# Two-layer encoder trunk on one core: weights of one recurrent output chunk by GpSimd alone, a join in pairs, a mean over four tiles

## The reference, cut to what matters

```
for i in range(2):
    a = rmsnorm(h, g[0])
    m = retention_mixer(a) if i == 0 else rglru_mixer(a)
    h = h + rmsnorm(m, g[1])
    f = conv_ffn(rmsnorm(h, g[2]))
    h = h + rmsnorm(f, g[3])
```

## Time and profile before

| what | us |
|---|---|
| median of 3 runs | 717.61 (717.42 to 718.76) |
| profiled execution, its time | 717.85 |
| profiled execution, its span | 716.0 |
| PE busy in the span | 704.6 |
| DVE busy | 607.3 |
| ACT busy | 520.2 |
| POOL busy | 25.0 |

### The profile page before, as it was taken

One profiled execution on the slowest core, in us unless ns is written; L12 is line 12 of the kernel. 1 busy time (PEld: TensorE's weight loads), 2 busy tenths in 40 slices (PEclk: granted clock), 3 DMA queues, 4 the chain that ended last, 5 costly groups with the idle time before them and its releaser, 6 DMA issues.

```text
span 716.0 us, 16121 instructions
## 1 busy us (share of the span) xinstructions
PE 704.6 (98%) x6542; PEld 589.9 (82%) x6542; DVE 607.3 (85%) x820; ACT 520.2 (73%) x848; POOL 25.0 (3%) x28
## 2 busy tenths in 40 slices
PE   9999999999999999999999999999899999999996
PEld 6788787878899888888889998888788888885464
DVE  6969877777889799989898889898999999999643
ACT  7566675857576789778777677899668888988431
POOL 0010010101010000000002300000000000000000
PEclk9999999999999999999999999999999999999999
DMA  9873363452683356555589963100525666766821
GB/s 309 318 234 120 119 235 119 166 188 104 211 274 121 111 192 225 192 195 200 176 264 388 370 216 117 62 1 1 196 98 190 224 206 207 233 211 207 275 43 59
DMA packets 106396, 132.08 MB, mean 184 GB/s; under 512 B 12385, under 2 KB 74337, under 8 KB 106209
## 3 DMA queue, kind: packets, MB, share of 16 engines
q1 hardware_dynamic: 105904, 130.97, 54.4%
q10 hardware_dynamic: 432, 0.31, 0.2%
HBM read 129.17 MB, written 1.05 MB: 182 GB/s over the span
## 4 chain that ended last, share of the span: by engine, by line
PE 82%; DVE 8%; ACT 6%; DMA 2%; issue 1%; SPq 1%; DVEq 0%
PE ps L1653 22%; PE ps L1655 22%; PE ps L1654 22%; PE ps L2036 3%; PE ps L2037 3%; PE ps L2035 3%; DMA stage<-in_ret_w_in 2%; PE ps L1696 1%; PE ps L1700 1%; PE ps L1695 1%; DVE a_lo L1082 1%; SPq L495 1%; PE ps L1901 1%; DVE hT L1098 1%; DVE w_lo L1036 1%
## 5 line engine op out<-in xcount | busy, mean ns | idle before, releaser
L1653 PE MATMUL ps<-a_hi,w_hi 128*128 128x272 f16 (+1 forms) x1000 | 276.9, 277 | 0.1
L1654 PE MATMUL ps<-a_lo,w_hi 128*128 128x272 f16 (+1 forms) x1000 | 276.9, 277 | 0.0
L1655 PE MATMUL ps<-a_hi,w_lo 128*128 128x272 f16 (+1 forms) x1000 | 276.9, 277 | 0.0
L1036 DVE SCALAR_TENSOR_TENSOR w_lo<-stage,w_hi 128x1024 f16<-128x1024 f32 x207 | 246.5, 1221 | 34.3 <-ACT w_hi L579 34.0
L579 ACT ACTIVATE w_hi<-stage 128x1024 f16<-128x1024 f32 x207 | 208.5, 1044 | 30.6 <-PE ps L2037 18.3
L1653 PEld LDWEIGHTS ps<-a_hi,w_hi 128*128 128x128 f16 x1000 | 97.8, 98 | 17.3 <-DVE rs L1045 0.9
L1655 PEld LDWEIGHTS ps<-a_hi,w_lo 128*128 128x128 f16 x1000 | 97.8, 98 | 16.0
L1654 PEld LDWEIGHTS ps<-a_lo,w_hi 128*128 128x128 f16 x1000 | 97.8, 98 | 15.7
L1653 PE MATMUL ps<-y_hi,w_hi 128*128 128x272 f16 (+3 forms) x496 | 106.1, 242 | 0.0
L1654 PE MATMUL ps<-y_lo,w_hi 128*128 128x272 f16 (+3 forms) x496 | 106.1, 242 | 0.0
L1655 PE MATMUL ps<-y_hi,w_lo 128*128 128x272 f16 (+3 forms) x496 | 106.0, 242 | 0.0
(11 more groups left out here) (278 smaller groups left out, 1104.2 us busy)
## 6 DMA issues: line engine op xcount, KB each, us to landing
stage<-in_ffn_w_in SPq DMA_DIRECT2D x96, 512.0 KB
stage<-in_ffn_w_out SPq DMA_DIRECT2D x24, 1024.0 KB
stage<-in_ret_w_in SPq DMA_DIRECT2D x16, 1024.0 KB
stage<-in_ret_w_out SPq DMA_DIRECT2D x8, 1024.0 KB
stage<-in_lru_w_in SPq DMA_DIRECT2D x8, 1024.0 KB
stage<-in_ret_w_in SPq DMA_DIRECT2D x12, 512.0 KB
stage<-in_lru_w_out SPq DMA_DIRECT2D x8, 512.0 KB
stage<-in_lru_w_a SPq DMA_DIRECT2D x8, 256.0 KB
```

Of the source, the lines that this page charges most:

```text
L1036: dve.scalar_tensor_tensor(out=part(1, c, q), in0=flat(stage, c, q), scalar=W_SCALE, in1=part(0, c, q), op0=ALU.mult, op1=ALU.subtract).th ...
L1653: pe.matmul(o, w_h, x_h, start=start, stop=False)
L1654: pe.matmul(o, w_h, x_l, start=False, stop=False)
L1655: return pe.matmul(o, w_l, x_h, start=False, stop=stop)
```

## The change

**Weights.** The four quarters of chunk `LRU_OUT` leave ACT's and DVE's `prep`. GpSimd makes them behind its last sum, in three instructions a quarter: the staged weights times 64 in place, a copy to f16 (high part), a subtraction (low part). Of the eight removed lines `prep(LRU_OUT, q)` one is shown below. GpSimd counts its quarters in a semaphore of its own, `pool_low`, on which PE waits for this chunk and SP for the load of `FFN1_IN`, the next user of that staging buffer. For this SP's loop over the chunks of the second FFN begins one round later, and the first round is written out. `whi_made` and `wlo_made` stay in step since the first quarter of `LRU_OUT + 1` adds five instead of one.

**Sum of four tiles.** In `residual_parts(1)` DVE leaves out the last two adds of squares, and the mean of the input norm of the recurrent layer sums tiles 0, 1, 4 and 5 on PE, in four products instead of one.

**Join in pairs.** In `residual(2, ...)` the output tiles are scaled by their gains on ACT, all eight, and the join goes in groups of one, one, two, two and two tiles in plain order.

```
+GROUPS = ((0, 1), (1, 1), (2, 2), (4, 2), (6, 2))
...
+        def counted(c, q):
+            return SUB + 1 if (c, q) == (LRU_OUT + 1, 0) else 1
...
+                        if isinstance(i, int) and c - 2 == LRU_OUT:
+                            sp.wait_ge(pool_low, 2 * half + 2)
+                        else:
+                            sp.wait_ge(wlo_made, SUB * (c - 2) + 2 * half + 2 + 2 * SUB * i)
...
+                if layer:
+                    for b in range(2):
+                        load_pair(first_in + b, ffn_w_in[layer], b * 2 * P, FFN + b * 2 * P)
+                with sp.Fori(layer, FFN_CHUNKS // 2) as i:
...
-            prep(LRU_OUT, 0)
...
+            def out_scaled(half, n):
+                act.activation(mT[:, half * 4 + n, T0_LRU_OUT:T], ps[:, (X, Y)[half] + n, T0_LRU_OUT:T], ACTF.Copy,
+                               scale=gain(5, half * 4 + n)).then_inc(m_part, 1)
             out_squares(LRU_OUT + 1, 2, 0, T0_LRU_OUT, 2)
-            out_squares(LRU_OUT + 1, 2, 1, T0_LRU_OUT)
+            out_scaled(0, 0)
+            out_scaled(0, 1)
+            out_square(LRU_OUT + 1, 2, 1, 0, T0_LRU_OUT)
+            out_scaled(0, 2)
+            out_square(LRU_OUT + 1, 2, 1, 1, T0_LRU_OUT)
+            out_scaled(0, 3)
+            out_square(LRU_OUT + 1, 2, 1, 2, T0_LRU_OUT)
+            out_square(LRU_OUT + 1, 2, 1, 3, T0_LRU_OUT)
+            for n in range(3):
+                out_scaled(1, n)
             estimate(STAT, T0_LRU_OUT, ms_up, MEAN[("post", 2)], ESTIMATE[("post", 2)])
+            out_scaled(1, 3)
...
-                link(dve.tensor_tensor(four, four, sq[:, 6:8, :], ALU.add))
-                link(dve.tensor_tensor(two, two, four, ALU.add))
-                dve.tensor_tensor(sq_sum[:], sq[:, 0, :], sq[:, 1, :], ALU.add).then_inc(sum_h, 1)
+                if i == 1:
+                    dve.tensor_tensor(four, four, sq[:, 6:8, :], ALU.add).then_inc(sum_h, 1)
...
+                for g in range(len(GROUPS) + 1):
+                    if g < len(GROUPS):
+                        dt, count = GROUPS[g]
+                        some = slice(dt, dt + count)
+                        dve.wait_ge(m_part, i * DT + dt + count)
+                        link(dve.tensor_tensor(mT[:, some, t0:T], mT[:, some, t0:T],
+                                               rs[:, t0:T].unsqueeze(1).to_broadcast([P, count, T - t0]), ALU.mult))
+                        dve.tensor_tensor(hT[:, some, t0:T], hT[:, some, t0:T], mT[:, some, t0:T],
+                                          ALU.add).then_inc(h_new, count)
+                    if g:
+                        before_dt, count = GROUPS[g - 1]
+                        for dt in range(before_dt, before_dt + count):
+                            norm_low(i + 1, dt, dt, t0)
...
-            out_scale(2, T0_LRU_OUT)
...
+            for q in range(SUB):
+                pool.wait_ge(w_landed[LRU_OUT % 2][q // 2], landed(LRU_OUT))
+                pool.wait_ge(w_used, freed(LRU_OUT, q))
+                raw = flat(stage, LRU_OUT, q)
+                link(pool.tensor_scalar(raw, raw, W_SCALE, None, ALU.mult))
+                link(pool.tensor_copy(part(0, LRU_OUT, q), raw))
+                pool.tensor_tensor(part(1, LRU_OUT, q), raw, part(0, LRU_OUT, q), ALU.subtract).then_inc(pool_low, 1)
...
+                        for dt in (0, 1, 4, 5):
+                            mm = pe.matmul(ps[:, STAT_IN[i], :T], ones_sb[:, 0, :], sq[:, dt, :], start=dt == 0, stop=dt == 5)
+                        mm.then_inc(ms_up, 1)
...
-                    pe.wait_ge(m_scaled, i + 1)
+                    pe.wait_ge(m_part, i * DT + 1)
...
+                    if c == LRU_OUT:
+                        pe.wait_ge(pool_low, q + 1)
```

More of the change, by code:

```diff
@@ L578, in prep @@
                     act.wait_ge(w_used, freed(c, q) + 2 * SUB * i)
-                act.activation(part(0, c, q), flat(stage, c, q), ACTF.Copy, scale=W_SCALE).then_inc(whi_made, 1)
+                act.activation(part(0, c, q), flat(stage, c, q), ACTF.Copy,
+                               scale=W_SCALE).then_inc(whi_made, counted(c, q))
             def estimate(bank, t0, up, n_up, n):
@@ L597, in norm_input @@
             def norm_input(i, t0, weights_after=()):
-                for n, dt in enumerate(JOIN_ORDER):
-                    act.wait_ge(h_new, (i - 1) * DT + n + 1)
+                for dt in range(DT):
+                    act.wait_ge(h_new, (i - 1) * DT + dt + 1)
                     high(i, dt, t0)
                     act.activation(sq[:, dt, t0:T], hT[:, dt, t0:T], ACTF.Square).then_inc(h_sq, 1)
-                    if n in weights_after:
-                        prep(FFN1_IN + 1, weights_after.index(n))
+                    if dt in weights_after:
+                        prep(FFN1_IN + 1, weights_after.index(dt))
             def norm_tokens():
@@ L1036, in prep @@
                 dve.scalar_tensor_tensor(out=part(1, c, q), in0=flat(stage, c, q), scalar=W_SCALE, in1=part(0, c, q),
[L1037 removed]
+                                         op0=ALU.mult, op1=ALU.subtract).then_inc(wlo_made, counted(c, q))
             def rsqrt(to, bank, t0, n):
@@ L1059, in out_scale @@
             def out_scale(i, t0):
-                for dt in range(4 if i < 2 else 2):
+                for dt in range(4):
                     dve.wait_ge(m_sq, i * DT + dt + 1)
-                    last = dve.tensor_scalar(mT[:, dt, t0:T], ps[:, (FULL + [X])[i] + dt, t0:T], gain(2 * i + 1, dt), None,
+                    last = dve.tensor_scalar(mT[:, dt, t0:T], ps[:, FULL[i] + dt, t0:T], gain(2 * i + 1, dt), None,
                                              ALU.mult)
@@ L1119, in residual_parts @@
                 dve.wait_ge(h_sq, (i + 1) * DT + 6)
-                mark(dve.tensor_tensor(two, two, sq[:, 2:4, :], ALU.add))
+                added = mark(dve.tensor_tensor(two, two, sq[:, 2:4, :], ALU.add))
                 part_low(i, 1, 3)
+                after(added)
                 dve.wait_ge(h_sq, (i + 2) * DT)
-                link(dve.tensor_tensor(four, four, sq[:, 6:8, :], ALU.add))
-                link(dve.tensor_tensor(two, two, four, ALU.add))
-                dve.tensor_tensor(sq_sum[:], sq[:, 0, :], sq[:, 1, :], ALU.add).then_inc(sum_h, 1)
+                if i == 1:
+                    dve.tensor_tensor(four, four, sq[:, 6:8, :], ALU.add).then_inc(sum_h, 1)
+                else:
+                    link(dve.tensor_tensor(four, four, sq[:, 6:8, :], ALU.add))
+                    link(dve.tensor_tensor(two, two, four, ALU.add))
+                    dve.tensor_tensor(sq_sum[:], sq[:, 0, :], sq[:, 1, :], ALU.add).then_inc(sum_h, 1)
@@ L1738, in chunk_normed @@
                 wh, wl = weights(c)
[L1739 to L1742, removed]
+                for k in range(KC):
+                    if k % 2 == 0:
+                        pe.wait_ge(wlo_made, SUB * c + k // 2 + 1)
+                    pe.wait_ge(ahi_made, NORM_BASE[i] + k + 1)
                     for n in range(4):
-                        if (at, n) == (0, 3):
-                            pe.wait_ge(h_new, (i - 1) * DT + 2)
                         col = slice(n * P, (n + 1) * P)
-                        pe.matmul(ps[:, X + n, t0:T], wh[:, k, col], a_hi[:, k, t0:T], start=at == 0, stop=False)
+                        pe.matmul(ps[:, X + n, t0:T], wh[:, k, col], a_hi[:, k, t0:T], start=k == 0, stop=False)
                         pe.matmul(ps[:, X + n, t0:T], wl[:, k, col], a_hi[:, k, t0:T], start=False, stop=False)
-                    pe.wait_ge(alo_made, NORM_BASE[i] + at + 1)
+                    pe.wait_ge(alo_made, NORM_BASE[i] + k + 1)
                     for n in range(4):
                         mm = pe.matmul(ps[:, X + n, t0:T], wh[:, k, n * P:(n + 1) * P], a_lo[:, k, t0:T],
[L1752 to L1755, removed]
+                                       start=False, stop=k == KC - 1)
+                    if k % 2 == 1:
                         mm.then_inc(w_used, 1)
@@ L1994, in _ @@
                         pe.wait_ge(gt_out, 2)
-                    pe.wait_ge(wlo_made, SUB * c + q + 1)
+                    if c == LRU_OUT:
+                        pe.wait_ge(pool_low, q + 1)
+                    else:
+                        pe.wait_ge(wlo_made, SUB * c + q + 1)
                     if half == 0:
```

12 lines of the change are left out of this document (2 added, 10 removed).

## The result

The changed kernel takes 730.73 us (median of 4 runs, 729.84 to 732.87) against 718.18 us for the kernel before on the same chip (4 runs): a ratio of 1.0179, 95% interval 1.0165 to 1.0194. The forecast was 728.0 us, slower, range 717.0 to 734.0. The profiled execution took 729.84 us, its span 727.8, which is 11.8 more than before.

A forecast was written before the change was run, and what follows sets the result against it. A late DVE in 423 to 447 us, then ACT from 455.44, was taken to bound the kernel. GpSimd's work with the four-tile sum +10.0, the second FFN's join +0.4: 717.6 + 10.4 = 728.0 us, range 717.0 to 734.0.

The forecast's parts named there:

- GpSimd's work in the join: First FFN's join: GpSimd's reads block DVE's two-input instructions, last a_lo 9.2 us late; gates +10.0 us including the four-tile sum.
- The price of a scaling: GpSimd's one-input scaling of 1024 f32 columns in place, taken as 1.09 us, between DVE's 0.72 and 2.34.
- my own rule: In the join, a blocked DVE loses GpSimd's working part: 0.9 us per scale or copy, 2.15 per subtraction.
- The 0.9 us that the prediction quotes for a one-input instruction: Estimate for 1024 columns on GpSimd, from the Trainium skill's 1.03 cycles a column at 1.2 GHz.
- Behind the join: From last a_lo to gates: late PE, mean and estimate, then GpSimd's remaining instructions; 9.2 us late becomes 10.0.
- Four-tile sum: Recurrent layer's input norm: PE's mean ends 1.35 us later, gates start 0.9 us late.
- Join: Ahead of the second FFN: PE waits some 0.5 us for a_lo of tiles 1 and 2, net +0.4 us.
- The unhindered case: Rival: GpSimd's work beside DVE costs nothing, leaving 0.9 + 0.4 = +1.3 us, 718.9; chance 0.14.
- Starving: Rival: GpSimd gets in only in DVE's true waits, PE waits for the first output quarter; near 730 us, chance 0.08.
- That one-input instructions don't block: Rival: only GpSimd's subtractions exclude DVE in the join; +7 us, 725 us, chance 0.15.
- The faster case: Rival: relieving DVE brings the recurrent chain forward and PE's output-block waits vanish; 715.3 us, chance 0.11.
- The low clock: Way to be wrong: granted clock, 0.998 before, falls in PE's idle stretch, adding time that the forecast didn't count.

The follow-up runs named there:

- pool_alone: Only GpSimd making the first output chunk's weights, put into the kernel before; sums and join as before: 730.18 us against 718.28, ratio 1.0171.
- join_and_four: The changed kernel without GpSimd's part, the chunk's weights on ACT and DVE again: 719.78 us against 718.28, ratio 1.0023.
- idle_reads: The kernel before, whole, plus the same twelve GpSimd instructions on idle memory, with nobody waiting for them before 470 us: 733.23 us against 718.02, ratio 1.0210.
- pool_late: The kernel before with GpSimd's part alone, started only once the fourth x_low is done: 726.57 us against 718.02, ratio 1.0123.
- prep_after_norm: The kernel before with DVE's prep of the chunk's first quarter moved behind x_evict, the second ahead of the third: 717.35 us against 717.88, ratio 0.9994.
- idle_writes: The kernel before, whole, plus twelve GpSimd memsets of 1024 f32 columns on idle memory: 718.31 us against 718.02, ratio 1.0009.
- the three starts tried here: GpSimd's part alone in the kernel before, started behind its last sum, after the first x_low, or after the fourth: 730.18, 726.25 and 726.57 us.

## Why the prediction was right

Direction, mechanism and place were right; sizes inside the sum were not, and partly cancelled.

*GpSimd's work in the join.* I had 6 short and 2 long instructions ahead of the last `a_lo`, 9.2 us. It was seven short ones and three long, 10.8 us. I had let GpSimd wait for DVE's pauses and had put the third subtraction and the fourth scaling behind the last `a_lo`, where DVE is free. In fact it waited once (the copy at 444.75, beside two preps back to back) and ran nose to tail else: also where DVE went from one instruction to the next over a semaphore that was already up. The two that came early are the 2.65 us at 439.87. Against that, a short one costs 0.71 to 0.84 instead of 0.9, and a subtraction 1.9 instead of 2.15.

*The price of a scaling* is the term that I had most wrong: 2.86 us against 1.09, outside my bounds (0.7 to 2.34), which assumed that two inputs can't be quicker than one. It cost little, since a scaling blocks DVE only for its first 0.8 us: in 430.71 to 432.3, in its second half, DVE's instructions have their old lengths (0.25 us at 430.71). That was luck. By my own rule, that a blocked DVE loses the whole working part, four scalings of 2.86 us instead of 1.09 would have added some 7 us to the sum, 735 us in all and outside my range. The rule fits the copy and the subtraction and fails for the scaling; why it lets DVE in after 0.8 us no run shows. The 0.9 us that the prediction quotes for a one-input instruction fits the copy, not the scaling.

*Behind the join.* I had 0.8 us more (10.0 after 9.2); measured is 0.5 more (11.3 after 10.8). The order was as forecast: the late `a_lo` delays PE, PE's mean of four starts at 446.99 instead of 436.69 and takes 1.4 us more, and DVE waits 2.48 us for the estimate. Then the first rsqrt step, at 449.55 beside GpSimd's last subtraction (448.05 to 450.17), took 0.92 instead of 0.43, the only loss behind the estimate where I had 1.65. I had PE done with XR1 0.5 us ahead of `x_low`; it was level with it. In `pool_alone` the gates were 12.0 late, 0.7 more than in the changed kernel: there the two stretched adds, 2.6 us longer than in before, make DVE late by itself. The granted clock fell there too (0.50 in 444 to 446 us, against 1.00 in the changed kernel), but DVE waits for nothing of PE's between the last `a_lo` and the rsqrt, and PE waits 0.3 us for DVE at the gates, so the clock doesn't make this difference.

*Four-tile sum.* Predicted +0.9 alone; measured +0.75 in the profile and +1.1 (0.2 to 1.9) in the times. The four products took 1.83 us, as I had them (4 x 0.45). `pool_alone` (+12.3) and `join_and_four` (+1.7) sum to 14.0, the whole change to 12.9: by the intervals they may simply add. The profiles say more: beside GpSimd the lean sum gave 0.7 us back at the gates, since it took two adds off a blocked DVE, where alone it cost 0.75.

*Join.* Predicted +0.4 (PE waits 0.5); PE waited 0.31 us at tile 2, and the times give +0.3 (-0.4 to +0.9). The reasoning held: `a_lo` of tile 2 came at 524.98 instead of 524.7, and PE wanted it at 524.73 instead of 524.3. The estimate had 1.04 us of cover, not the 0.3 that I counted.

*Rivals.* The unhindered case is out by `idle_reads` and by the stretched DVE rows of the changed kernel. Starving occurred once (3.21 us), and in `pool_late`, where GpSimd took 30 us. That one-input instructions don't block is out: the copy costs DVE 0.71 us in each of the three times that it met the join. The faster case had its chance in `prep_after_norm`: relief of DVE ahead of rsqrt shows 0.6 us in its profile and nothing clear in the times. The low clock, which I named as a way to be wrong, did occur; its price is 0.9 to 1.7 us by the two ways of counting and not clear of nothing.

The rule of the Trainium skill that I leaned on (SBUF — State Buffer, "Who interferes with whom") holds here in what it says of reads and of two SBUF inputs: `idle_writes` is free, `idle_reads` is not. Where it says that whoever issues first holds the shared pair for the whole instruction (said there of DVE's 2-port modes), GpSimd's scaling differs: 2.86 us long, 0.7 to 0.8 us blocked.

## What to carry to other kernels

An engine that is 3% busy isn't free: before work goes to GpSimd, look at what DVE does at that time, and count each GpSimd instruction that reads SBUF as time taken from the DVE instructions with two SBUF inputs beside it, here 3.4 us a quarter against the 1.13 that DVE saved. A burst of GpSimd work must land where DVE truly idles, and a share of busy time doesn't show that: the three starts tried here cost 12, 8.5 and 8.8 us. If GpSimd must help beside a dense DVE, give it what only writes, as the memsets here.

## What the runs showed of the hardware that I hadn't expected

- GpSimd's scaling of 1024 f32 columns in place takes 2.77 to 2.88 us in the changed kernel, more than its two-input subtraction (2.12 to 2.28 us) and more than its copy to f16 (1.06 to 1.09 us where unhindered), and blocks DVE only 0.7 to 0.8 us of it.
- A DVE instruction is held up though it has no pause before it: the multiply at 423.27 follows `a_lo` directly and takes 0.84 us more.
- DVE's scaling of 1088 f32 columns (one SBUF input, 0.72 us in the earlier trace rows) is slowed too: in `pool_late` it took 2.65 us. Timeline of DVE:

```profile
481.52 2.65 DVE L1452 TENSOR_SCALAR work<-work 128x1088 f32<-128x1088 f32 x1
```

- The granted clock fell to 0.50 after one PE wait of 3.0 us in the changed kernel, but not after the wait of 3.3 us that ends at 443.1. In `pool_alone`, with nearly the same waits, it did fall after the second: 0.50 in 444 to 446 us. In before it stayed at 1.00 in every stretch of 422 to 448 us.
